# Norm vectors turned once and spread by TensorE, turned keys kept, the output projection between the heads, and a last norm moved behind the dots

## The reference

```python
def rms_norm(x, g):
    y = x * rsqrt(mean(x * x, axis=-1) + EPS)
    return y * g

def odd_mixer(x, ...):                        # layer 1
    h = rms_norm(x, norm_g)
    cq, k, v, ik, iw = split(h @ w_in)
    uq = rms_norm(cq, g_qa) @ w_uq
    q, iq = split(uq)                         # 16 heads of 128, 16 index heads of 64
    score = einsum(iw, relu(iq @ ik.T))       # top 64 keys of each token are kept
    o = softmax(mask(q @ k.T * dh ** -0.5)) @ v
    return x + o @ w_out

def peer_ffn(h, w_q, sub_keys, u, v):         # both layers, per block of 128 tokens
    q = (h @ w_q).reshape(128, 8, 2, 128)
    s = einsum('thcd,hcnd->thcn', q, sub_keys)
    # per token and head the 16 best of 128 * 128 experts -> eidx (8 * 16), softmax -> g
    act = gelu(einsum('thkd,td->thk', u[eidx], h))
    return einsum('thk,thkd->td', g * act, v[eidx])

# per layer: x = mixer(x); x = x + peer_ffn(rms_norm(x, g_ffn), ...); at the end rms_norm(x, norm_final)
```

## Time and profile before

| | |
|---|---|
| median of 3 runs | 3349.12 us (3348.32 to 3352.23) |
| the profiled execution | 3349.19 us, its span 3347.3 us |
| VectorE (DVE) busy | 2373.4 us, 71% |
| TensorE (PE) busy | 1691.0 us, 51%, mean granted clock 0.794 |
| GpSimd (POOL) busy | 1553.7 us, 46% |
| ScalarE (ACT) busy | 334.9 us, 10% |
| DMA | 1288.28 MB, mean 385 GB/s over the span |
| gathers | 1074.86 MB of it, the loads and stores of SyncE's queue 212.37 MB |

### The profile page before, as it was taken

How to read it: one execution, slowest core, us unless ns; L and a number is a source line. 1 busy time by engine, 2 the same in 40 slices (tenths; PEclk the granted TensorE clock), 3 DMA queues, 4 the chain that set the end, 5 groups by cost and what they waited for, 6 DMA issues and landing times.

```text
span 3347.3 us, 17715 instructions
## 1 busy us (share of the span) xinstructions
PE 1691.0 (51%) x4964; PEld 854.1 (26%) x4964; DVE 2373.4 (71%) x2749; ACT 334.9 (10%) x778; POOL 1553.7 (46%) x1042
## 2 busy tenths in 40 slices
PE   7999957520777662646477763464477710000000
PEld 3687653210222231312222232322122200000000
DVE  1012397689777478957877577967786689999998
ACT  1111100000111101101111112201011100000000
POOL 0012154368666445725656454634566633333332
PEclk9999979875999986688799977697899965555555
DMA  6343699999999999999999999899999999999997
GB/s 229 126 151 139 244 414 421 422 422 421 422 421 414 420 416 418 394 416 421 422 422 419 417 419 417 351 417 421 422 421 422 422 422 422 422 422 422 422 422 321
DMA packets 210009, 1288.28 MB, mean 385 GB/s; under 512 B 22784, under 2 KB 22784, under 8 KB 64128
## 3 DMA queue, kind: packets, MB, share of 16 engines
q0 software_dynamic: 147728, 1074.86, 77.6%
q1 hardware_dynamic: 62192, 212.37, 16.2%
HBM read 1285.05 MB, written 2.10 MB: 385 GB/s over the span
## 4 chain that ended last, share of the span: by engine, by line
issue 28%; POOL 22%; DMA 19%; PE 16%; DVE 12%; ACT 2%; DVEq 0%; POOLq 0%; SPq 0%; ACTq 0%; PEldq 0%
POOL ring L481 22%; DMA ring<-in_peer_v,eidx 12%; DVE ps L1243 9%; PE ps L864 5%; DMA ring<-in_peer_u,eidx 5%; PE ps L740 5%; PE ps L724 4%; DMA HT<-in_peer_wq 2%; DVE X L1243 1%; PE ps L720 1%; ACT KT L595 0%; PE ps L885 0%; DVE A L1140 0%; ACT A L595 0%; DVE kdup L1234 0%
## 5 line engine op out<-in xcount | busy, mean ns | idle before, releaser
L481 POOL DMA_INDIRECT ring<-in_peer_u,eidx x512 | 796.8, 1556 | 835.9 <-DVE dots L1234 657.8
L1234 DVE CUSTOM_DVE_ANT_0 kdup<-ring,H 128x2048 bf16<-128x2048 f32 x384 | 880.0, 2292 | 264.6 <-DMA ring<-in_peer_u,eidx 257.9
L481 POOL DMA_INDIRECT ring<-in_peer_v,eidx x512 | 725.1, 1416 | 636.8 <-DVE ps L1243 187.2
L1243 DVE SCALAR_TENSOR_TENSOR X<-ring,wgt,X 128x1024 f32<-128x1024 f32 (+1 forms) x384 | 548.6, 1429 | 301.2 <-DMA ring<-in_peer_v,eidx 292.7
L864 PE MATMUL ps<-ring,KT 128*128 128x512 f32 x672 | 332.4, 618 | 247.6 <-DMA ring<-in_peer_v,eidx 177.2
L864 PE MATMUL ps<-ring,A 128*128 128x512 f32 x656 | 326.5, 623 | 172.8 <-DMA ring<-in_peer_v,eidx 105.0
L1243 DVE SCALAR_TENSOR_TENSOR ps<-ring,wgt,ps 128x2048 f32<-128x2048 f32 x128 | 301.5, 2355 | 20.3 <-DVE ps L1243 6.0
L1234 DVE CUSTOM_DVE_ANT_0 kdup<-ring,ps 128x2048 bf16<-128x2048 f32 x128 | 292.8, 2287 | 16.9 <-DMA ring<-in_peer_u,eidx 9.9
L864 PEld LDWEIGHTS ps<-ring,KT 128*128 128x128 f32 x672 | 115.8, 191 | 462.8 <-issue 281.5
L864 PEld LDWEIGHTS ps<-ring,A 128*128 128x128 f32 x656 | 114.4, 193 | 384.2 <-issue 205.9
L740 PE MATMUL ps<-HT,ring 128*128 128x256 f32 x768 | 169.6, 382 | 1.3 <-ACT PR L607 1.3
(11 more groups left out here) (237 smaller groups left out, 1738.4 us busy)
## 6 DMA issues: line engine op xcount, KB each, us to landing
ring<-in_w_in SPq DMA_DIRECT2D x18, 2048.0 KB, 9.0
PR<-in_peer_wq SPq DMA_DIRECT2D x32, 1024.0 KB, 16.1
PR<-in_w_out SPq DMA_DIRECT2D x24, 1024.0 KB, 16.1
ring<-in_w_out SPq DMA_DIRECT2D x8, 2048.0 KB, 8.0
A<-in_peer_wq SPq DMA_DIRECT2D x16, 1024.0 KB, 16.1
A<-in_w_out SPq DMA_DIRECT2D x12, 1024.0 KB, 16.1
HT<-in_peer_wq SPq DMA_DIRECT2D x8, 1024.0 KB, 16.1
ring<-in_peer_u,eidx POOLq DMA_INDIRECT x512, 17.0
```

The costliest lines, as they stand in the source:

```text
L481: pool.indirect_dma_start(ring[:, n % RING, :], None, table, bass.IndirectOffsetOnAxis(eidx[:, b, n:n + 1], 0)).then_inc(landed[n % RING], 16)
L1234: V.tensor_tensor_reduce(out=junk, in0=ring[:, s % RING, :], in1=last_h if phase == 6 else H[:, b, :], scale=1.0, scalar=0.0, op0=ALU.mult ...
L1243: V.scalar_tensor_tensor(out=acc, in0=ring[:, s % RING, 0:cols], scalar=weight, in1=acc, op0=ALU.mult, op1=ALU.add).then_inc(ring_free, 1)
```

## The change

Three of the five norm vectors (layer 1's two and the final one) are no longer copied to all partitions. Each is loaded once at the start as 16 rows of 128 values (`gain_rows`), turned by TensorE into 16 columns (`gainT`), and before a norm spread to all partitions in four PSUM banks by 16 matmuls of a column, repeated, with the identity (`spread_gain`). For the last block's norm of block 0 (`norm(7)`) and for the last norm of all ScalarE copies the spread vector into SBUF (`last_gain`, in HT). `norm(7)` and its squares now stand behind phase 6 instead of ahead of it, and so does the store of block 0's output.

The freed tile `gain` holds the router's turned keys of layer 1 for both blocks, so their load and their transposes are made for b = 0 alone.

The attention of layer 1 uses one pair of banks for all that a group does (`pair(q)`, banks 0 and 1 or 2 and 3), banks 4 to 7 take the output projection, and TensorE runs a quarter of it (4 weight rows) behind each group of heads. Pieces 8 to 11 stand at places 15, 17, 19, 21 instead of 14 to 17, pieces 12 and 13 at 24 and 25 instead of 25 and 27; routing's pieces stand up to two places earlier.

The last slot of phase 7 is added in two halves of 1024 columns. Each half is squared once it is there, and the last norm and its store are made in halves.

The diff in its core, in the order SyncE, ScalarE, TensorE, VectorE behind the tiles:

```diff
-    (name, b, n) for b in (0, 1) for name, n in (..., ("keys1", 4), ...)]
+    (name, b, n) for b in (0, 1) for name, n in (..., ("keys1", 4 * (1 - b)), ...)]
...
-        PKT1 = PR[:, 2048:4096].rearrange("p (g n) -> p g n", n=NKEY)
+        PKT1 = gain[:, :].rearrange("p (g n) -> p g n", n=NKEY)
+        gain_rows = MTf[0:KT_, 2048:2048 + 3 * P].rearrange("p (i n) -> p i n", n=P)
+        last_gain = HTf[:, 0:2048]
...
+        def pair(q):
+            return bank(2 * (q % 2), 2)
...
+            for i in range(3):
+                sp.dma_start(gain_rows[:, i, :], gains[2 + i].rearrange("(k p) -> k p", p=P)).then_inc(rows_loaded, 16)
...
             for b in range(NB):
                 sp.wait_ge(routed, b + 2)
-                load_gain(3 + 2 * b)
...
-                load_gain(4 + 2 * b)
...
                 sp.wait_ge(pv_done, 8 + 4 * (b + 1))
-                sp.dma_start(PKN1, ...).then_inc(keys1_loaded, 16)
+                if b == 0:
+                    sp.dma_start(PKN1, ...).then_inc(keys1_loaded, 16)
                 load_rows("wq1", b, peer_wq1, rows_l1)
-            load_gain(7)
-            for b in range(NB):
-                sp.wait_ge(h_ready, norm_before(8 + b))
-                sp.dma_start(out[0, b * P:(b + 1) * P, :], H[:, b, :]).then_inc(out_stored, 16)
+            sp.wait_ge(h_ready, norm_before(8))
+            sp.dma_start(out[0, 0:P, :], H[:, 0, :]).then_inc(out_stored, 16)
+            for i in range(2):
+                cols = slice(i * 1024, (i + 1) * 1024)
+                sp.wait_ge(half_ready, i + 1)
+                sp.dma_start(out[0, P:T, cols], H[:, 1, cols]).then_inc(out_stored, 16)
...
             act.wait_ge(merged, 3)
-            squares(7)
             for c in range(4):
                 nc.scalar.copy(bank(4 + c), X[:, 1, c * CH:(c + 1) * CH]).then_inc(lifted, 1)
             gelus(1, 1)
-            act.wait_ge(ring_free, RING + 8 * SLOTS)
-            nc.scalar.activation(H[:, 1, :], last_x, ACT.Square, accum_out=stat[:, 0, 1:2]).then_inc(sq_done, 1)
+            act.wait_ge(gain_spread, 5)
+            for c in range(4):
+                nc.scalar.copy(last_gain[:, c * CH:(c + 1) * CH], bank(c)).then_inc(lifted, 1)
+            squares(7)
+            for i in range(2):
+                act.wait_ge(half_summed, i + 1)
+                nc.scalar.activation(H[:, 1, i * 1024:(i + 1) * 1024], last_x[:, i * 1024:(i + 1) * 1024], ACT.Square,
+                                     accum_out=halves[:, i:i + 1]).then_inc(sq_done, 1)
...
+            def spread_gain(i, bank0):
+                for k in range(KT_):
+                    at = bank0 * 512 + k * P
+                    last = nc.tensor.matmul(ps[:, at:at + P], gainT[:, i, k:k + 1].broadcast_to([P, P]), ident[:, :],
+                                            start=True, stop=True)
+                last.then_inc(gain_spread, 1)
...
+            def attention1(b):
+                n, q0 = tiles_before("out1", b), 8 + 4 * b
+                scores(1, q0)
+                for g in range(4):
+                    if g < 3:
+                        scores(1, q0 + g + 1)
+                    values(1, q0 + g)
+                    pe.wait_ge(pv_copied, q0 + g + 1)
+                    for k in range(4 * g, 4 * g + 4):
+                        pe.wait_ge(s_loaded[n % WSLOTS], 16 * (n // WSLOTS + 1))
+                        for c in range(4):
+                            last = nc.tensor.matmul(bank(4 + c), MT1[:, k, :], rows_l1[n % WSLOTS][:, c * CH:(c + 1) * CH],
+                                                    start=(k == 0), stop=(k == KT_ - 1))
+                        last.then_inc(s_used, 1)
+                        n += 1
+                chunk_ends(s_used, WSLOTS + n)
...
-                attention(1, 8 + 4 * b, 4)
-                whole_rows("out1", b, rows_l1, MT1)
-                pe.wait_ge(keys1_loaded, 16 * (b + 1))
-                pe.wait_ge(chunk_added, added_after("out1", b))
-                transpose_stage("keys1", b)
+                attention1(b)
+                spread_gain(1, 0)
+                if b == 0:
...
+            pe.wait_ge(dots_ready, 4)
+            spread_gain(2, 0)
...
-            MIX_AT = (0, 4, 7, 8, 11, 12, 13, 14, 15, 16, 17, 25, 27)
-            OUT_AT = (5, 6, 8, 9, 11, 12, 14, 16, 18, 20, 22, 24, 26)
+            MIX_AT = (0, 4, 7, 8, 11, 12, 13, 15, 17, 19, 21, 24, 25)
+            OUT_AT = (4, 5, 7, 8, 10, 11, 13, 15, 17, 19, 21, 23, 25)
...
-            norm(7)
             dve.wait_ge(lifted, 4)
             expert_dots(1, 1, 6)
             dve.wait_ge(lifted, 8)
+            norm(7)
             expert_sum(1, 7)
-            norm(8)
+            last_norm()
```

More of the change, by code:

```diff
@@ L826, in values @@
                 pe.wait_ge(pt_copied, q + 1)
-                if q >= 2:
+                if layer == 0 and q >= 2:
                     pe.wait_ge(pv_copied, q - 1)
@@ L1280, in expert_sum @@
                 else:
-                    with dve.Fori(0, PEER_H) as i:
+                    with dve.Fori(0, PEER_H - 1) as i:
                         for s in range(PEER_K):
                             weigh(b, phase, i, s, wgt[:, bass.ds(i * PEER_K + s, 1)])
+                    for n in range(SLOTS - PEER_K, SLOTS - 1):
+                        weigh(b, phase, n // PEER_K, n % PEER_K, wgt[:, n:n + 1])
+                    last_weigh(phase)
                 dve.wait_ge(ring_free, (phase + 1) * SLOTS + RING)
```

107 lines of the change are left out of this document (77 added, 30 removed).

## The result

The changed kernel takes 3335.68 us, the median of 6 runs (3334.35 to 3336.56), against 3349.41 us of the kernel before (6 runs): the ratio is 0.9957, with a 95% interval of 0.9945 to 0.9968. It is faster by 13.7 us; 17.6 were forecast. The profiled execution took 3336.56 us with a span of 3334.8 us, 12.5 us less than the span of before.

The account below looks back on a forecast made before the run. Bytes at 422 GB/s plus DMA starvation bound it up to the last dot, then one VectorE chain. 3349.2 - 18.5 (bytes) - 10 (starvation) + 0.5 (start) + 12 (hand-over) - 1.7 (tail) = 3331.5 us; range 3318 to 3346.

Parts of the forecast that it names:

- Bytes: Up to the last dot: copies, keys and store leaving the full DMA stretch gain 18.5 us at 422 GB/s.
- The copies: Five norm-vector copies to all partitions, 1 MiB each, leave SyncE's queue: 12.4 us gained.
- the keys: Block 1's load of the router's keys, 1 MiB in 512 B pieces, goes: 3.6 us gained.
- the store: Block 0's output store leaves the stretch before the last dot: 2.5 us gained, returning in phase 7 at no cost.
- The start: Small loads, three transposes and a copy added at the start cost 0.5 us (between 0 and 1).
- Starvation: DMA engines starving in both blocks' attention stretches: 10 of 20.4 us come back, 9.5 of them from 2120 to 2180.
- Rival (a): Starvation stays, VectorE's new waits at places 17 and 19 replacing the old one at 2142: 3341.5 us; chance 16%.
- (b): More comes back: all 20.4 us of starvation go (3321), or the hand-over is mostly hidden (3323); chance 13%.
- The wait of 6 us at places 17 and 19: In attention, VectorE waits some 6 us for scores, a 26 us chain against 20 us between pieces; counted as hidden.
- The hand-over: Between last dot and phase 7's first sum: spreading, copies and `norm(7)` delay the first sum 12 us (8 to 17).
- The tail: At the end, the last sum, squares and store in halves save 1.7 us (between 0 and 3).
- Rival (c): Slower: between head groups TensorE waits for the quarters' weight rows and the ring starves, 36 us lost: 3378; chance 8%.

Follow-up runs that it names:

- experiment 10: The kernel before without the five copies of norm vectors to all partitions behind the start: 3336.29 us (0.9959).
- experiment 11: The kernel before without block 1's load of the router's keys, the transposes staying: 3345.62 us (0.9988).
- experiment 12: The kernel before with block 0's output store waiting for the last dot: 3349.14 us (0.9999).
- experiment 4: The changed kernel with the output projection whole again behind the attention, new places and bank pairs kept: 3349.40 us (0.9999).
- experiment 8: The changed kernel with the tail whole again (one last sum, one row of squares, one product, one store): 3336.29 us (0.996).
- experiment 1: The changed kernel with the final vector spread and copied in phase 5 and `norm(7)` ahead of phase 6 again: 3323.42 us (0.9921).
- experiment 3: The changed kernel with VectorE's and routing's pieces back at the old places, the projection's quarters kept: 3345.88 us (0.9989).
- experiment 7: The changed kernel with the early spread and norm of experiment 1, plus pieces 3 to 6 at places 6, 7, 9, 11: 3320.84 us (0.9915).

## Why the prediction was right, point by point

**Bytes: 18.5 forecast, 17.4 left over in the account of the traces.** The copies and the keys stand by experiments 10 and 11 (12.1 to 13.7 for 12.4, and 3.5 to 4.4 for 3.6; the lower reading of each is the trace's, the higher the medians'). Of the store, the forecast said that it comes back in phase 7 and costs nothing there. That holds for the changed kernel, with its long hand-over; with the short one it costs phase 7 1.8 us of waits for landings (experiment 12).

**The start: 0.5 forecast, 0.9 measured** in this pair of traces. The first dot stands at 409.1 to 410.3 in the five traces of kernels with the old start and at 409.4 to 410.2 in the nine with the new one, 0.5 us apart in the mean.

**Starvation: 10 forecast, 7.6 measured.** The step was right for the windows that it named: from 2140 on 418 and 420 GB/s. Too much was taken back in 2120 to 2140 (397 against 385 before, where 422 was assumed), and block 0's stretch gave 0.8 of 1. A second reading agrees: from the first maximum of block 1's attention to the `wgt` copy it takes 883.4 us against 898.4; 8.6 of these 15.0 us are bytes (one copy, the keys, the store), so 6.4 are block 1's starvation, for 9.5 forecast. That the new waits of 6.8 and 2.1 us are hidden is shown by the same windows. Why the starvation goes is only half as forecast: the forecast's balance of 20.1 us of VectorE against 19.9 of gathers is enough to fill the engines (experiment 4, 417 GB/s with no weight row in flight), while the flowing rows cover VectorE's waits for the matmuls and bring the projection in time. Rival (a) is refuted, and so is the part of (b) that had all starvation go.

The wait of 6 us at places 17 and 19 was forecast with a misread row. The 9.68 us of the projection's row were taken for the sixteen matmuls of a quarter; they are eight, for each is listed twice (see the hand-over). In the changed kernel a quarter is 32 rows and takes 13.8 us, from 2135.76 to 2149.60, at the higher clock:

```profile
2135.76 7.13 PE L902 MATMUL ps<-PR,MT 128*128 128x512 f32 x16 [0.68 <-ACT MT L592]
2142.73 3.60 PE L902 MATMUL ps<-A,MT 128*128 128x512 f32 x8
2146.17 3.60 PE L902 MATMUL ps<-MT 128*128 128x512 f32 x8
```

The scores behind it take 3.65 us in place of 5.5, TensorE's clock being up by then, and the chain from the reciprocal at 2126.27 to the maximum at 2153.25 is 27.0 us, for 26 forecast. That the sum came out is luck.

**The hand-over: 12 forecast, 14.65 measured, the largest error.** The mis-sized term is the spreading. It was priced by 16 transposes, 3.65 us, and took 6.52; copies and norm were priced right (8.4 less 6.5 is 1.9 for the copies, forecast 2.13; the norm 6.25, forecast 6.66). The trace lists each of these matmuls twice, x32 for 16, as it does those of the projection, where the 16 transposes of the same size are listed once: a product of float32 values stands in this trace as two rows, a transpose as one. The same 32 rows take 3.81 us where TensorE has been at work:

```profile
1467.52 3.81 PE L736 MATMUL ps<-ident,gainT 128*128 128x128 f32 x32
```

Windows around that row and around the hand-over's (the last three numbers are the granted clock, the DMA share and GB/s):

```profile
1467.00:1472.00 5.00, 4.17 (x33) 3.65 (x32) 2.30 (x2) 0.00 (x0) 1.87 (x2) 1.00 1.01 422
2990.00:2996.00 6.00, 5.99 (x29) 6.00 (x30) 0.29 (x1) 0.21 (x1) 0.53 (x1) 0.53 1.02 425
```

The spreading at 2990.01 follows 319 us in which TensorE did nothing, at a granted clock of 0.53, so nearly all of it at the lower level, 1.2 GHz; at 1467 the clock is 2.4 GHz. The forecast had the clock right and the form wrong. (How soon the clock rises differs between executions: in the six traces with this hand-over the gap is 14.7 to 15.9 us, and in the shortest, experiment 8, the spreading takes 5.36. In the first 5 us of the hand-over the granted clock is 0.67 there and 0.50 in the changed kernel.) Rival (b)'s hidden hand-over is refuted by the rows: in the written order all waits for the last dot.

**The tail: -1.7 forecast, -3.1 measured** (with 0.7 us of it in the gaps ahead of the last slot, from a cause that no run shows). The halves were right, 1.5 us. What the forecast did not see is that moving `norm(7)` behind the gelu takes the table load out of the tail, worth 0.8 us on the chain; experiment 1, which moves it back, gets the load back. The Trainium skill has this effect in "ScalarE: Activation LUTs", "Table sets: the hidden batching unit": functions of different sets cost a load each time they alternate, and this trace agrees, with one load of 1.28 us fewer at the end. No run here shows a drain on top of a load: at the hand-over the root starts 0.02 us behind the 1.28 us of the load.

**Rival (c)** had the right kind of danger and the wrong place. In the changed kernel no quarter waits for its weight rows, and in experiment 3 they cost TensorE 1.3 us; VectorE's waits for the matmuls between the groups starve the ring only where the pieces stand closer than the chain is long (experiment 3), and there they cost 10 us against the changed kernel, not 47.

The errors of these five terms, 1.1, 0.4, 2.4, 2.65 and -1.4, add up to 5.15 us; the profiled execution took 3336.56, 5.1 more than the 3331.5 forecast. Start, starvation and hand-over lie inside their stated bounds, the tail at the edge of its (3), and the bytes had none. The forecast was right in its accounts and their signs; that the total was off by 5 us and not by less or more is no finding, for the traces themselves scatter by 1 to 3 us.

**A version that beats both** is the changed kernel with experiment 1, with or without experiment 7: 3323.4 and 3320.8 us, 0.9921 and 0.9915 of the kernel before.

## What to carry to other kernels

Where a program changes from a stretch set by bytes to one serial chain, small work belongs ahead of the change, where the ring covers it: the norm and its spreading delay the last dot by 1.0 us there and the first sum by 14.65 here. A schedule's table and the work between its places are one edit: each half of this one made the kernel slower by itself, one because a piece then stood ahead of the work that it waits for, so a test of one half says nothing of the pair. Before a row is used as a price, count the program's instructions in it: that matmuls of float32 stand there twice was missed in two places here, and made the largest error in one and a lucky sum in the other. And a transfer taken away pays only what its neighbours leave it: price it in the kernel in which it will be gone.

## What was not expected of the hardware

- Sixteen float32 matmuls of a repeated column with the identity are listed as 32 and take 6.52 us at the lower clock and 3.81 at the higher, where 16 transposes of the same shape at the lower clock take 3.65.
- ScalarE's table is still there after some 320 us: the root at 3328.11 loads nothing, its table having been loaded at 3000.53.
- In the changed kernel the DMA engines' pause at the hand-over (251 GB/s from 2996 to 3006, 4 us lost) is never seen by VectorE: its sums stay at 2.51 us. Without the pause, a store of 1 MiB at the start of phase 7 makes two sums wait for landings (experiments 1 and 12).
- A table load of 1.28 us in front of the last root costs the chain 0.6 to 0.8 us, since VectorE's two small steps run beside it.
